# Which engine issues the stores of the squared hidden layer in a hybrid decoder step

## The chip, the cores and the metric

The kernel runs on one core of a Trainium2 chip. The metric is the device time of one execution in microseconds (us), as the median of several runs. The engines are PE (TensorE: matmuls, with PEld for its weight loads), DVE (VectorE), ACT (ScalarE), POOL (GpSimd) and SP (SyncE, which here only waits and issues DMAs). Each engine works off its own list of instructions in order, and an instruction that waits holds back all behind it on that engine. Waits are on semaphores.

## The reference, cut to what matters

One inference step of a one-layer decoder, for 512 prompt tokens and 8 sample tokens, 520 columns in all, with a model width D of 2048: sparse attention and retention side by side, an output projection, then a squared-ReLU MLP and a last RMSNorm. The change lies in the MLP:

```
u = rmsnorm(x, norm2_g) @ w_up            # w_up 2048 x 8192
x = x + jnp.square(jax.nn.relu(u)) @ w_down   # w_down 8192 x 2048
return rmsnorm(x, final_norm_g)
```

All data are float32. Precision is kept by splitting each operand of a product in a high part (a rounded copy, `_hi`, fp32r) and a low part (the rest, `_lo`); a product is three matmuls: hi by hi, hi by lo, lo by hi.

## The kernel before, in words

**The up-projection** goes in 32 groups (g = 0 to 31, `UPG` = 32) of 256 hidden units. The 2 x 2 block product (two halves of the 2048 inputs by two halves of the units, for two halves of 260 tokens) is done with seven products in place of eight, after Strassen and Winograd: DVE makes sums of weight blocks (`sum_blocks`, in PSUM tiles "banks"), and the results are combined afterwards. So a group (from group 1 on) has seven positions, 0 to 6. Each is 24 matmuls of 128 x 260 on PE (`product`, line 907). For each position ACT casts the weights to `w_hi` (`high_unit`, line 1206), and POOL (positions 0, 1, 5, line 578) or DVE (2, 3, 4, 6: `low_sum`, line 1795) subtracts to get `w_lo`.

**PSUM banks** of a group: position 0 writes bank 2 or 0 (by the parity of g), and position 2 adds to the same bank once ACT has copied what position 0 left there (`taken(g, 0, ...)`, line 1251, into `c_b`). PE waits for that copy ahead of position 2 (`s_ra`). The last product of a group is read by ACT's Relu into `r21` at the start of the next group.

**The squares.** After group g - 1, and so during group g, ACT makes the Relus and squares (`relu_rest`, `squared`), DVE combines them to seven block combinations `h_f` (`combine_hidden`, lines 1815 to 1818), ACT makes `h_hi` (`hidden_high`, line 1278) and DVE, last in its list of the group, `h_lo` (`hidden_low`, line 1825). Each of these is 128 x 1820 numbers. Both are then stored to DRAM (`hidden_combinations`, two DMAs of 910 KB) by `store_hidden`. `s_hl` counts the `h_lo` that are done, `s_store` the stores that have landed (32 a group). ACT's `hidden_high(g)` waits for the stores of group g - 1 to have landed, since `h_hi` is a single buffer.

**SP's list** in the up-projection, for each g from 1: wait that a raw buffer is free and load the first half of the weights of group g + 1 (`half_free`, `load_half`, line 430; 1 MB), the same for the second half, then `store_hidden(g - 1)`: wait for `s_hl` and issue the two stores (lines 478 and 479). After group 31's round come seven pairs of loads of stored squares for the first chunk of the down-projection (`load_hidden(0, pos)`, line 490, into `s_dn`, which lies where the normed x, `s_up`, was, so that each waits for PE's use of positions in group 31), a load of weights, `store_hidden(31)`, another load of weights, seven pairs for the second chunk, and, once all stores have landed, the reload of x (line 516) into the space that also held `h_f`, `h_hi` and `h_lo`.

**The down-projection** has 32 groups (g = 32 to 63): 8 chunks of 1024 hidden units by 4 groups of 512 output columns, with seven positions each, of two times 12 matmuls. DVE adds every result to x (`add_down`, line 1865); from the second group on these adds need the x reloaded last.

**ACT's list** in group g: the cast for position 2, Relu of `r21`, Relu of `c_b`, the cast for position 3, the three squares, the copy of `c_b` from position 0, the casts for 4 and 5, a copy, the cast for 6, a copy, the cast for position 0 of group g + 1, `hidden_high(g - 1)`, the cast for position 1 of group g + 1. The functions at the heart of it, as the kernel before has them:

Of the kernel before, what the change touches and what calls it, by code (L numbers as in the profile page):

```python
# [45 lines left out]
UPG, DNG = DFF // HB, NCHUNK * (D // 512)  # L46
# [9 lines left out]
F32, F32R, BF16, I32 = mybir.dt.float32, mybir.dt.float32r, mybir.dt.bfloat16, mybir.dt.int32  # L56
# [10 lines left out]
def base_unit(g):  # L67

    return TAKEN0_UNITS + (4 + 7 * (g - 1) if g else 0)


def ring_slot(n):

    down = base_unit(UPG)
    if n >= down:
        order = (1, 2, 0, 3)
        k = n - down
        return order[k % 4], n - 4 if k >= 4 else (n - 3 if k < 3 else None)
    k = n - TAKEN0_UNITS
    return (k + 2) % 3, n - 3 if k >= 3 else (130, 132, 133)[k]  # L80


def raw_slot(j):

    return (j + 1) % RAWS, 16 * (j // RAWS + 1)
# [38 lines left out]
def build(nc, x_prompt, x_sample, cache_k, cache_v, cache_idx_k, state_ret, page_table, norm1_g, w_in,  # L124
# [3 lines left out]
    with ctx:  # L128
        BASE = 16512

        def at(name, offset, shape, dt=F32):
            return nc.alloc_sbuf_tensor_at(name, shape, dt, offset=BASE + offset)
# [29 lines left out]
        h_hi = at("h_hi", R0 + 11392 + 7296, [P, 7, HALF_COLS], F32R)  # L162
        h_lo = at("h_lo", R0 + 11392 + 14592, [P, 7, HALF_COLS], F32R)
# [108 lines left out]
        h_dram = nc.dram_tensor("hidden_combinations", (P, UPG, 2, 7, HALF_COLS), F32).ap()  # L272
# [4 lines left out]
        def block_of(g, i, j):  # L277

            slot, _ = raw_slot(2 * g + i)
            if g < UPG:  # L280
                return raw[:, slot, :].rearrange("p (k c) -> p k c", c=2 * P)[:, :, j * P:(j + 1) * P]
            return raw[:, slot, :].rearrange("p (k c) -> p k c", c=4 * P)[:, :, 2 * j * P:2 * (j + 1) * P]

        def sums_in(g, n):

            if g < UPG:
                return (T0, T1)[n]
            if g >= LAST_CHUNK and n == 0:
                return t_s[:, :, :]
            return (T0W, T1W)[n]  # L290

        def ring(w, g, n):
            slot, _ = ring_slot(n)
            x = w[:, slot, :, :]
            return x if g < UPG else x.rearrange("p k c -> p (k c)").rearrange("p (k c) -> p k c", c=2 * P)
# [4 lines left out]
        def last_x(g):  # L300

            return 2 if g % 2 else 0
# [54 lines left out]
        def _(sp):  # L357
# [61 lines left out]
            def load_half(g, i):  # L419

                slot, _ = raw_slot(2 * g + i)
                if g < UPG:
                    dst = raw[:, slot, :].rearrange("p (k c) -> p k c", c=2 * P)
                    src = w_up[1024 * i:1024 * i + 1024, HB * g:HB * g + HB].rearrange("(k p) c -> p k c", p=P)
                else:
                    c, w = divmod(g - UPG, D // 512)
                    dst = raw[:, slot, :].rearrange("p (k c) -> p k c", c=4 * P)
                    src = w_down[1024 * c:1024 * c + 1024, 512 * w:512 * w + 512].rearrange(
                        "(k two p) c -> two p k c", two=2, p=P)[i]
                sp.dma_start(dst, src).then_inc(s_h[slot], 16)  # L430

            def half_free(g, i):

                if 2 * g + i < 2:
                    return
                if 2 * g + i == 2:
                    sp.wait_ge(s_lo, TAKEN0_UNITS)
                    return
                before, which = divmod(2 * g + i - RAWS, 2)
                if before == 0:  # L440
                    sp.wait_ge(s_lo, pool_lows(0, 2 + 2 * which))
                elif which == 0:
                    sp.wait_ge(s_lo, pool_lows(before, 1))
                    sp.wait_ge(s_t, 4 * (before - 1) + 3)
                else:
                    sp.wait_ge(s_lo, pool_lows(before, 3))
                    sp.wait_ge(s_t, 4 * (before - 1) + 4)
# [24 lines left out]
            half_free(1, 1)  # L472
            load_half(1, 1)

            def store_hidden(g):

                sp.wait_ge(s_hl, g + 1)
                sp.dma_start(h_dram[:, g, 0, :, :], h_hi[:, :, :].bitcast(F32)).then_inc(s_store, 16)
                sp.dma_start(h_dram[:, g, 1, :, :], h_lo[:, :, :].bitcast(F32)).then_inc(s_store, 16)

            def load_hidden(c, pos):

                if c >= 2:
                    sp.wait_ge(s_used, base_unit(UPG + 4 * (c - 2) + 3) + pos + 1)
                else:
                    sp.wait_ge(s_used, base_unit(UPG - 1) + (pos // 2, (7 + pos) // 2)[c] + 1)
                if c >= 1:
                    sp.wait_ge(s_sd[pos], 32 * c)
                for n in range(2):
                    sp.dma_start(s_dn[:, c % 2, pos, n, :, :].bitcast(F32),  # L490
                                 h_dram[:, 4 * c:4 * c + 4, n, POS_STORE[pos], :]).then_inc(s_sd[pos], 16)

            for g in range(1, UPG):
                half_free(g + 1, 0)
                load_half(g + 1, 0)
                half_free(g + 1, 1)
                load_half(g + 1, 1)
                store_hidden(g - 1)
                if g == UPG - 4:
                    for n in range(2):  # L500
                        sp.wait_ge(s_xs[n], 16 * (5 - n))
                    sp.wait_ge(s_slp, 2)
                    sp.wait_ge(s_sl, 7)
                    sp.dma_start(xr[:, 0:5, :], x2_dram[:, 0:5, :]).then_inc(s_xl[0], 16)
# [2 lines left out]
                load_hidden(0, pos)  # L507
            half_free(UPG + 1, 0)
            load_half(UPG + 1, 0)
            store_hidden(UPG - 1)  # L510
            half_free(UPG + 1, 1)
            load_half(UPG + 1, 1)
            for pos in range(7):
# [519 lines left out]
        def _(act):  # L1033
# [154 lines left out]
            def high_unit(g, pos):  # L1188

                n = base_unit(g) + pos  # L1190
                _, before = ring_slot(n)
                if before is None:
                    act.wait_ge(s_sqh, UPG)
                else:
                    act.wait_ge(s_used, before + 1)
                raw_of = {0: (0, 0), 1: (0, 1), 2: (1, 0), 3: (1, 1)} if g == 0 else {0: (0, 0), 1: (1, 0), 5: (1, 1)}
                if pos in raw_of:
                    i, j = raw_of[pos]
                    slot, loaded = raw_slot(2 * g + i)
                    act.wait_ge(s_h[slot], loaded)  # L1200
                    x = block_of(g, i, j)
                else:
                    which, summed = {2: (1, 2), 3: (0, 1), 4: (0, 3), 6: (1, 4)}[pos]
                    act.wait_ge(s_t, 4 * (g - 1) + summed)
                    x = sums_in(g, which)
                nc.scalar.copy(ring(w_hi, g, n), x).then_inc(s_hi, 1)  # L1206
# [39 lines left out]
            def taken(g, pos, dst, b, fn=None):  # L1246

                act.wait_ge(s_used, base_unit(g) + pos + 1)
                act.wait_ge(s_sqh, g)
                src = G[:, b, 0:HALF_COLS]  # L1250
                (act_fn(dst, src, fn) if fn else nc.scalar.copy(dst, src)).then_inc(s_ra, 1)

            def relu_rest(g):

                act.wait_ge(s_rv, 3 * g)
                act_fn(c_b[:, :, :], c_b[:, :, :], ACT.Relu).then_inc(s_r0, 1)
# [16 lines left out]
            def hidden_high(g):  # L1273

                act.wait_ge(s_comb, g + 1)
                if g:
                    act.wait_ge(s_store, 32 * g)
                nc.scalar.copy(h_hi[:, :, :], h_f[:, :, :]).then_inc(s_hh, 1)

            for g in range(1, UPG):  # L1280
                x_bank = last_x(g)
                high_unit(g, 2)
                if g > 1:
                    taken(g - 1, 6, r21[:, :], last_x(g - 1), ACT.Relu)
                    relu_rest(g - 1)
                high_unit(g, 3)
                squared(g - 1)
                taken(g, 0, c_b[:, 0, :], x_bank)
                high_unit(g, 4)
                high_unit(g, 5)  # L1290
                taken(g, 2, c_b[:, 1, :], x_bank)
                high_unit(g, 6)
                taken(g, 3, c_b[:, 2, :], 3)
                high_unit(g + 1, 0)
                hidden_high(g - 1)
                high_unit(g + 1, 1)
            g = UPG
            taken(g - 1, 6, r21[:, :], last_x(g - 1), ACT.Relu)
            high_unit(g, 2)
# [1 line left out]
            squared(g - 1)  # L1301
            high_unit(g, 3)
            hidden_high(g - 1)

            def squares_of(i):

# [684 lines left out]
```

## Time and profile before

| | us |
|---|---|
| median of 3 runs (2442.13 to 2445.2) | 2444.73 |
| the profiled execution, its own time | 2438.56 |
| its span in the profile | 2436.8 |
| PE busy with matmuls (share of the span) | 2330.6 (96%) |
| DVE / ACT / POOL busy | 1595.0 / 937.6 / 869.7 |
| mean granted clock of PE | 0.975 |

All numbers of the profile belong to the one profiled execution; times are counted from its span's start. A line number names a line of the kernel. "SPq" and "ACTq" are the lists of SP and ACT as far as they issue DMAs, which isn't counted as busy time. A granted clock of 1.00 is PE's upper level of 2.4 GHz, 0.50 its lower one of 1.2 GHz. In the chain of waits "issue" is time in which the engine waited for nothing that the profile shows.

### The profile page before, as it was taken

The numbers are of one execution on the slowest core, as the hardware profiler recorded it, in microseconds if no ns is written. First come the engines' busy times: TensorE is split into PE (matmuls) and PEld (weight loads), VectorE is DVE, ScalarE is ACT, GpSimd is POOL, SyncE is SP. The second block draws the span as 40 slices with busy tenths as digits, with TensorE's granted clock in tenths as the row PEclk, the third lists the DMA queues.
The fourth block names the chain that finished last, engine by engine and source line by source line (L and its number), as shares of the span: only waits on it lengthen the run. The fifth ranks groups of instructions, "written<-read, shape, count | busy, mean of one in ns | idle before, by whom it ended". The sixth has DMA issues, their size and how long they took to land.

```text
span 2436.8 us, 46019 instructions
## 1 busy us (share of the span) xinstructions
PE 2330.6 (96%) x18396; PEld 2257.3 (93%) x18396; DVE 1595.0 (65%) x2316; ACT 937.6 (38%) x1213; POOL 869.7 (36%) x357
## 2 busy tenths in 40 slices
PE   8999999999999999889999999998599999999996
PEld 8969899999999899889999999998599999999996
DVE  5368625555555643488888888888377777777764
ACT  5241222222222322245555555555133333333343
POOL 3413323332333444243333333333133333333353
PEclk9999989999999999899999999999799999999998
DMA  6523223333333443325555555565935556555621
GB/s 217 141 65 102 80 73 89 91 91 91 87 87 86 147 121 113 112 66 197 197 197 197 197 197 197 197 210 201 372 106 192 192 175 227 192 192 175 227 87 71
DMA packets 347063, 368.77 MB, mean 151 GB/s; under 512 B 16594, under 2 KB 301458, under 8 KB 345746
## 3 DMA queue, kind: packets, MB, share of 16 engines
q1 hardware_dynamic: 334850, 352.16, 45.3%
q10 hardware_dynamic: 12064, 14.53, 1.6%
q8 instruction: 105, 1.72, 0.3%
q14 instruction: 44, 0.36, 0.0%
HBM read 288.85 MB, written 77.80 MB: 150 GB/s over the span
## 4 chain that ended last, share of the span: by engine, by line
PE 90%; DVE 4%; DMA 2%; issue 2%; ACT 1%; SPq 1%; POOL 0%; ACTq 0%; DVEq 0%
PE product L907 51%; PE product L618 31%; PE banks L649 6%; PE banks L646 1%; DVE s_up L1738 1%; DMA raw<-in_w_down_dram 1%; DMA x_in<-in_x_prompt_dram 1%; DMA raw<-in_w_up_dram 0%; PE product L649 0%; DVE xr L1732 0%; DMA s_dn<-hidden_combinations 0%; DVE a_lo L1687 0%; SPq L490 0%; DVE xr L1756 0%; DVE score L1504 0%
## 5 line engine op out<-in xcount | busy, mean ns | idle before, releaser
L578 POOL TENSOR_TENSOR w_lo<-raw,w_hi 128x1024 fp32r<-128x1024 f32 x193 | 499.7, 2595 | 852.7 <-ACT w_hi L1206 852.0
L907 PE MATMUL product<-s_dn,w_hi 128*128 128x260 f32 x3584 | 662.8, 287 | 38.0 <-DVE xr L1865 25.1
L907 PE MATMUL product<-s_up,w_hi 128*128 128x260 f32 x3600 | 653.9, 284 | 17.1 <-ACT c_b L1042 8.0
L907 PEld LDWEIGHTS product<-s_dn,w_hi 128*128 128x128 f32 x3584 | 561.8, 191 | 41.7 <-issue 33.7
L907 PEld LDWEIGHTS product<-s_up,w_hi 128*128 128x128 f32 x3600 | 556.8, 189 | 21.5 <-issue 14.2
L545 POOL TENSOR_TENSOR w_lo<-w_raw,w_hi 128x1024 fp32r<-128x1024 f32 (+1 forms) x134 | 323.6, 2417 | 659.0 <-ACT w_hi L1039 658.9
L907 PE MATMUL product<-s_dn,w_lo 128*128 128x260 f32 x1792 | 511.4, 285 | 0.0
L907 PE MATMUL product<-s_up,w_lo 128*128 128x260 f32 x1800 | 508.5, 282 | 0.0
L618 PE MATMUL product<-a_hi,w_hi 128*128 128x260 f32 (+1 forms) x2144 | 440.1, 286 | 7.8 <-DVE a_lo L1396 3.9
L618 PE MATMUL product<-a_hi,w_lo 128*128 128x260 f32 (+1 forms) x2144 | 433.7, 284 | 0.0
L618 PE MATMUL product<-a_lo,w_hi 128*128 128x260 f32 (+1 forms) x2144 | 432.8, 284 | 0.0
L1206 ACT CAST w_hi<-banks 128x1024 fp32r<-128x1024 f32 x244 | 247.6, 1015 | 468.6 <-PE product L907 242.9
L1039 ACT CAST w_hi<-w_raw 128x1024 fp32r<-128x1024 f32 (+1 forms) x134 | 139.6, 1043 | 576.5 <-PE product L618 427.6
L1795 DVE TENSOR_TENSOR w_lo<-banks,w_hi 128x1024 fp32r<-128x1024 f32 x244 | 298.0, 1221 | 74.9 <-ACT w_hi L1206 74.0
L618 PEld LDWEIGHTS product<-a_hi,w_hi 128*128 128x128 f32 (+1 forms) x2144 | 331.8, 189 | 15.2 <-issue 8.1
L907 PEld LDWEIGHTS product<-s_dn,w_lo 128*128 128x128 f32 x1792 | 342.2, 191 | 0.0
L907 PEld LDWEIGHTS product<-s_up,w_lo 128*128 128x128 f32 x1800 | 340.4, 189 | 0.0
L618 PEld LDWEIGHTS product<-a_hi,w_lo 128*128 128x128 f32 (+1 forms) x2144 | 331.5, 189 | 0.0
L618 PEld LDWEIGHTS product<-a_lo,w_hi 128*128 128x128 f32 (+1 forms) x2144 | 330.6, 188 | 0.0
L1865 DVE TENSOR_TENSOR xr<-xr,product 128x260 f32<-128x260 f32 x448 | 188.0, 421 | 181.4 <-PE product L907 157.6
L1206 ACT CAST w_hi<-raw 128x1024 fp32r<-128x1024 f32 x193 | 202.8, 1051 | 233.7 <-PE product L907 200.5
L1789 DVE TENSOR_TENSOR banks<-banks,raw 128x1024 f32<-128x1024 f32 x122 | 149.4, 1224 | 6.0 <-DMA raw<-in_w_down_dram 5.3
(270 smaller groups left out, 1905.9 us busy)
## 6 DMA issues: line engine op xcount, KB each, us to landing
raw<-in_w_up_dram SPq DMA_DIRECT2D x64, 1024.0 KB, 9.6
raw<-in_w_down_dram SPq DMA_DIRECT2D x64, 1024.0 KB, 5.3
s_dn<-hidden_combinations SPq DMA_DIRECT2D x112, 520.0 KB, 8.7
w_raw<-in_w_in_dram SPq DMA_DIRECT2D x100, 512.0 KB, 3.8
hidden_combinations<-h_hi SPq DMA_DIRECT2D x32, 910.0 KB, 3.8
hidden_combinations<-h_lo SPq DMA_DIRECT2D x32, 910.0 KB, 6.8
w_raw<-in_w_out_dram SPq DMA_DIRECT2D x32, 512.0 KB, 4.0
x_transposed<-xr ACTq DMA_DIRECT2D x2, 2080.0 KB, 7.6
```

Of the source, the lines that this page charges most:

```text
L545: nc.gpsimd.tensor_tensor(w_lo[:, slot, :, 0:cols], w_raw[:, raw, :, 0:cols], w_hi[:, slot, :, 0:cols].bitcast(F32), ALU.subtract).then_in ...
L578: nc.gpsimd.tensor_tensor(ring(w_lo, g, n), block_of(g, i, j), ring(w_hi, g, n).bitcast(F32), ALU.subtract).then_inc(s_lo, 1)
L618: last_mm = nc.tensor.matmul(out[:, half, :], w[:, slot, k, 0:cols], a[:, k0 + k, half * HT:(half + 1) * HT], start=(first and k == 0 and ...
L646: return nc.tensor.transpose(out, x, ident[0:n, 0:n])
L649: return nc.tensor.matmul(out, lhsT, rhs, start=start, stop=stop, skip_group_check=True)
L907: mm_last = nc.tensor.matmul(out, w[:, k, col:col + P], s[:, h, k, :], start=(first and k == 0 and part == 0), stop=(last and k == kn - 1 ...
L1039: nc.scalar.copy(w_hi[:, n % RING, :, 0:cols], w_raw[:, n % 2, :, 0:cols]).then_inc(s_hi, 1)
L1206: nc.scalar.copy(ring(w_hi, g, n), x).then_inc(s_hi, 1)
L1738: v.tensor_tensor(s_up[:, pos, 1, ks, :], x[:, ks, :], s_up[:, pos, 0, ks, :].bitcast(F32), ALU.subtract).then_inc(s_sl, 1)
L1789: v.tensor_tensor(out, x, y, ALU.add).then_inc(s_t, 1)
L1795: v.tensor_tensor(ring(w_lo, g, n), sums_in(g, (k + 1) % 2), ring(w_hi, g, n).bitcast(F32), ALU.subtract).then_inc(s_lt, 1)
L1865: v.tensor_tensor(acc, acc, G[:, 2 * sub + pos % 2, 0:HALF_COLS], op).then_inc(s_rd, 1)
```

## The change

`store_hidden` moves from SP's list to ACT's, with its wait and both DMAs. In group g ACT now ends its list, after the cast for position 1 of group g + 1, with `store_hidden(g - 1)`; the last, `store_hidden(31)`, follows `hidden_high(31)`, ahead of the casts of group 32's position 4 and later. SP's list keeps its order without these entries. Nothing else is changed.

```
@@ SP's list
-            def store_hidden(g):
-
-                sp.wait_ge(s_hl, g + 1)
-                sp.dma_start(h_dram[:, g, 0, :, :], h_hi[:, :, :].bitcast(F32)).then_inc(s_store, 16)
-                sp.dma_start(h_dram[:, g, 1, :, :], h_lo[:, :, :].bitcast(F32)).then_inc(s_store, 16)
-
...
                 half_free(g + 1, 1)
                 load_half(g + 1, 1)
-                store_hidden(g - 1)
                 if g == UPG - 4:
...
             half_free(UPG + 1, 0)
             load_half(UPG + 1, 0)
-            store_hidden(UPG - 1)
             half_free(UPG + 1, 1)
             load_half(UPG + 1, 1)
@@ ACT's list
                 nc.scalar.copy(h_hi[:, :, :], h_f[:, :, :]).then_inc(s_hh, 1)
 
+            def store_hidden(g):
+
+                act.wait_ge(s_hl, g + 1)
+                act.dma_start(h_dram[:, g, 0, :, :], h_hi[:, :, :].bitcast(F32)).then_inc(s_store, 16)
+                act.dma_start(h_dram[:, g, 1, :, :], h_lo[:, :, :].bitcast(F32)).then_inc(s_store, 16)
+
...
                 hidden_high(g - 1)
                 high_unit(g + 1, 1)
+                store_hidden(g - 1)
             g = UPG
...
             high_unit(g, 3)
             hidden_high(g - 1)
+            store_hidden(g - 1)
```

## Rows read from the trace of the kernel before

**Rows 1.** The page's busy table: us (share of the span), instructions of each engine.

```profile
PE 2330.6 (96%) x18396; PEld 2257.3 (93%) x18396; DVE 1595.0 (65%) x2316; ACT 937.6 (38%) x1213; POOL 869.7 (36%) x357
```

**Rows 2.** The chain that ended last: start us, us, what.

```profile
1072.90 546.95 PE product L907 x4536
...
1748.92 16.99 issue
```

**Rows 3.** Stretches: us, busy us (instructions) by engine, granted clock, DMA share, GB/s.

```profile
1087.47:1107.72 20.25, 20.25 (x170) 20.12 (x170) 17.52 (x17) 11.95 (x16) 7.85 (x4) 1.00 0.59 197
...
1699.80:1765.90 66.10, 32.35 (x216) 31.80 (x216) 19.53 (x29) 10.34 (x11) 7.12 (x3) 0.73 1.06 369
```

**Rows 4.** Timeline, SP and ACT at the hand-over: start, us, engine, line, [idle before <-releaser].

```profile
1679.92 3.76 SPq L430 DMA_DIRECT2D raw<-in_w_down_dram  x2
...
1696.17 0.39 ACT L1042 ACTIVATE r<-product 128x260 f32<-128x260 f32 x1 [1.81 <-PE product L907]
...
1699.78 21.16 SPq L490 DMA_DIRECT2D s_dn<-hidden_combinations  x14
...
1724.92 26.76 SPq L490 DMA_DIRECT2D s_dn<-hidden_combinations  x14
...
1751.73 1.41 SPq L516 DMA_DIRECT2D xr<-x_after_attention  x1
```

**Rows 5.** Timeline of the engines at one boundary of groups, 1103 to 1114 us.

```profile
1103.15 5.46 POOL L578 TENSOR_TENSOR w_lo<-raw,w_hi 128x1024 fp32r<-128x1024 f32 x2 [3.33 <-ACT w_hi L1206]
...
1106.37 4.15 DVE L1825 TENSOR_TENSOR h_lo<-h_f,h_hi 128x1820 fp32r<-128x1820 f32 x1
...
1107.76 1.01 ACT L1206 CAST w_hi<-banks 128x1024 fp32r<-128x1024 f32 x1 [1.81 <-PE product L907]
1108.67 0.39 ACT L1042 ACTIVATE r<-product 128x260 f32<-128x260 f32 x1
...
1110.62 1.02 ACT L1206 CAST w_hi<-banks 128x1024 fp32r<-128x1024 f32 x1 [0.82 <-PE product L907]
...
1111.46 4.06 SPq L430 DMA_DIRECT2D raw<-in_w_up_dram  x2
...
1112.88 0.38 ACT L1251 COPY c_b<-product 128x260 f32<-128x260 f32 x1
...
1113.17 0.28 PE L907 MATMUL product<-s_up,w_lo 128*128 128x260 f32 x1
1113.40 0.48 PE L907 MATMUL product<-s_up,w_hi 128*128 128x260 f32 x2
```

**Rows 6.** Line 1825, h_lo: count, duration in ns min/median/max, first and last start.

```profile
L1825 DVE TENSOR_TENSOR h_lo<-h_f,h_hi x32: 2044/4142/4149, 1086.1 to 1707.7; 128x1820 fp32r<-128x1820 f32 x32
```

**Rows 7.** Waits from 1072.9 to 1696.1, SP and PE: us, times, longest.

```profile
SPq L478 <- DVE h_lo L1825: 456.3, 30, 15.4
...
PE product L907 <- ACT c_b L1251: 2.3, 1, 2.3
```

**Rows 8.** Timeline of ACT about its own output stores in the attention stage.

```profile
388.51 0.37 ACTq L1162 DMA_DIRECT2D out_dram<-rst  x1
...
389.46 1.28 ACT L1042 ACT_TABLE_LOAD   x1 [0.88 <-issue]
```

**Rows 9.** Stretches at gaps of PE, columns as in group 3.

```profile
1072.90:1076.31 3.41, 3.41 (x28) 3.41 (x29) 2.28 (x3) 1.29 (x2) 0.00 (x0) 1.00 0.19 50
...
2365.69:2368.30 2.61, 0.00 (x0) 0.03 (x1) 1.11 (x3) 1.40 (x4) 0.00 (x0) 1.00 0.75 290
2368.30:2371.71 3.41, 3.41 (x16) 3.33 (x17) 0.00 (x0) 1.54 (x3) 1.98 (x2) 0.51 0.00 0
```

**Rows 10.** The chain again: 24 products after gaps of PE, and undisturbed.

```profile
2369.56 3.92 PE product L907 x24
...
2374.03 2.89 PE product L907 x24
...
2396.09 4.30 PE product L907 x24
```

More of the change, by code:

```diff
@@ L473, in _ @@
             load_half(1, 1)
[L475 to L479, printed above, removed]
             def load_hidden(c, pos):
@@ L497, in _ @@
                 load_half(g + 1, 1)
-                store_hidden(g - 1)
                 if g == UPG - 4:
@@ L509, in _ @@
             load_half(UPG + 1, 0)
-            store_hidden(UPG - 1)
             half_free(UPG + 1, 1)
@@ L1278, in hidden_high, with store_hidden @@
                 nc.scalar.copy(h_hi[:, :, :], h_f[:, :, :]).then_inc(s_hh, 1)
+            def store_hidden(g):
+                act.wait_ge(s_hl, g + 1)
+                act.dma_start(h_dram[:, g, 0, :, :], h_hi[:, :, :].bitcast(F32)).then_inc(s_store, 16)
+                act.dma_start(h_dram[:, g, 1, :, :], h_lo[:, :, :].bitcast(F32)).then_inc(s_store, 16)
             for g in range(1, UPG):
@@ L1296, in _ @@
                 high_unit(g + 1, 1)
+                store_hidden(g - 1)
             g = UPG
@@ L1303, in _ @@
             hidden_high(g - 1)
+            store_hidden(g - 1)
             def squares_of(i):
```

## The prediction

> **What bounds the kernel now.** I read the page's busy table first. The matmuls of TensorE (PE) are busy for 96% of the span, and no other engine above 65% [rows 1]. The chain of waits then says where PE is left alone. One piece of it is 546.95 us of products from 1072.90 on, without a gap: nearly the whole up-projection, the stage in which the squares are stored. In the hand-over to the down-projection the same chain is broken, longest by "issue 16.99" from 1748.92 to 1765.91, a stretch in which the view names nobody [rows 2].
>
> The change touches both places, so I asked of each what ends last there. In the hand-over it is the memory: from 1699.80 to 1765.90 the DMA engines have a share of 1.06 at 369 GB/s [rows 3], and PE stands again when x comes back, whose reload was issued last, at 1751.73, behind 28 loads of stored squares [rows 4]. In the steady groups I laid the engines' own rows beside each other at one boundary: ACT's first cast of the new group follows PE's last unit of the old one at 1107.76 [rows 5]. A group takes 20.25 us, with PE busy for 20.25 [rows 3].
>
> **What SP is relieved of.** In the up-projection SP stood 30 times and 456.3 us in all for DVE's h_lo, ahead of the store of h_hi [rows 7]: 15.2 us in each group. The loads queued behind it were not late for PE, since nothing in that piece of the chain waits for them [rows 2]. In the steady groups this removes idle time of an engine with slack, and I cost it at nothing.
>
> **What ACT takes on.** The wait moves with its two issues. ACT now stands, at the end of each group's list, for the h_lo of the group before. Behind it is queued the next group's list: the cast for position 2, Relu of r, Relu of c_b, the cast for position 3, three squares, and the copy of c_b that frees the PSUM bank which PE writes again at position 2.
>
> When is h_lo ready? DVE starts it at 1106.37 and it takes 4.15 us, so it ends at 1110.52 [rows 5], 2.76 us after ACT began the new group. That is every group's case: of 32 such instructions the median takes 4142 ns, and the shortest 2044 [rows 6]. It is long because POOL's two subtractions run until 1108.61 [rows 5]; from there to 1110.52 it is 1.91 us, close to the short form. Both POOL pieces follow casts that ACT does ahead of the new wait, so I leave the end at 1110.52.
> The Trainium skill, "SBUF — State Buffer" (section "SBUF: two separate sides"), says that a VectorE instruction with two SBUF inputs waits wholly while a GpSimd instruction reads SBUF: a lock, not a shared bandwidth. The trace agrees: with half the rate during the 2.24 us of overlap h_lo would have taken 3.2 us, not 4.15. By shared bandwidth the stall below would be 0.95 us smaller.
>
> What do the issues cost? From h_lo's end at 1110.52 SP needs until 1111.46 to come to its next load, signal and both stores included: 0.94 us [rows 5]. ACT's own pair of output stores, at 388.51, lets its next instruction begin at 389.46: 0.95 us [rows 8]. I take 0.94.
>
> So ACT begins the group at 1111.46 and not at 1107.76: 3.70 us late. What covers it? ACT idled 0.82 us ahead of the cast for position 3, and an instruction with nothing to wait for starts 0.1 us before the last one ends (1108.67 against 1107.76 + 1.01) [rows 5]: 0.9 us together. There is no second reserve. The copy of c_b runs from 1112.88 to 1113.26, and PE's position 2 began at 1113.40, 0.23 us after the matmul before it, where 0.12 is the usual distance [rows 5]: PE already waits 0.11 us for this copy. What is beyond the 0.9 us is PE's idle time: 3.70 - 0.90 = 2.8 us. DVE's w_lo for position 2 would be ready at 1111.46 + 1.01 + 1.2 = 1113.7 and is not the later one. After position 2 the group moves as one: h_lo hangs on PE's position 5, through DVE's work on c_b, so the next boundary finds the same distances and nothing is made up.
>
> The stores of groups 0 to 29 delay groups 2 to 31: 30 x 2.8 = 84 us. The bounds for one group are 0, if ACT finds a cover that I don't see, and 3.70, if none of the 0.9 us can be used; I take 2.8, since each piece has its row, with 2.5 to 3.0 about it.
>
> **The clock.** PE's gap becomes 2.8 + 0.11 = 2.9 us in each group of about 23. The trace has gaps near that. After one of 2.61 us at 2365.69 the granted clock was 0.51 over the next 3.41 us (and the same came after its twin at 2392.60), but in the up-projection it was 1.00 after a gap of 2.3 us [rows 9], which is the very wait in question: PE for the copy of c_b, in the first group [rows 7]. After the two falls 24 products took 3.92 and 4.30 us instead of 2.89 [rows 10], dearer by 1.03 and 1.41, on average 1.2. With two of three gaps followed by the lower level, 1.2 GHz, that is 0.8 us a group and 24 us in all. Bounds: 0, and half of 3.41 us, 1.7, in every group, 51 us.
>
> **The hand-over.** SP passes straight from the loads of group 32's weights to the loads of the squares. The last of the former was issued by 1679.92 + 3.76 = 1683.68, the first of the latter at 1699.78, after SP's wait for h_lo [rows 4], 16.1 us apart. Their own condition, that PE has used positions of group 31, is met by then or a few us on, and they read groups 0 to 3, stored long before. The stretch is one of bandwidth and 66.1 us long. It begins 16.1 us earlier against PE's end of group 31 and has one load of 1 MB more inside, 2.8 us at 369 GB/s: a gain of 13.3, say 13. What is late next? ACT comes into the stretch 3.7 us late, and its last h_hi waits until the store of group 30 has landed, which now runs beside loads. By the durations above, position 2 of group 32 starts 15 to 20 us after PE's end of group 31 (that was about 1696.1, when `r<-product` starts on ACT [rows 4]), with some 20 us of products to go before x is needed. x comes at 56 us (1765.9 - 1696.1 - 13), so this is covered. Bounds for the gain: 0 and 20.
> The Trainium skill, "DMA: Bandwidth & Descriptors" ("Issuing engines are not separate DMA queues"), says that DMAs of different engines interleave on the same 16 engines, so that a second issuer only saves time on the first one's sequencer. By that rule the second queue adds no bandwidth and the gain is that of the order alone. No row before the change has stores of ACT beside saturated loads of SP. Its section on the anatomy of a DMA adds that a semaphore wait is made on the issuing sequencer: SP's 456.3 us are such waits, and they are what speaks against ACT as the issuer.
>
> **The sum**, against the profiled execution (2438.56 us, span 2436.8): 84 + 24 - 13 = +95, that is 2533.6. The median of the three timed runs lies 6.2 us higher, at 2444.73. With that difference: 2540 us.
>
> **Rivals.**
> (a) The stall comes, and the clock stays high, as after the 2.3 us gap: +84 - 13 = +71, 2516. For it speaks that one case; against it, that the new gap is longer than all three.
> (b) The clock falls in every group: +84 + 51 - 13 = +122, 2567. Against it: both prices read are under 1.7.
> (c) The other side: the wait on ACT is covered and only the hand-over changes, 2444.7 - 13 = 2432. Its one mechanism is that h_lo is done before ACT comes to the store. To cost nothing it must end by 1107.76 + 0.9 - 0.94 = 1107.7, 2.8 us sooner than now. Against it: even the short form, from 1106.37, ends at 1108.4, and would leave 0.7 us a group (+21 - 13 = +8).
> (d) The change does nothing: the loads of squares stay where they are, and the wait on ACT is short. 2445; the rows name no cause for either.
>
> **Chances.** The forecast 0.62 (its own range 2525 to 2560), (a) 0.20, (b) 0.12, (c) 0.04, (d) 0.02. The range that should hold 8 in 10 reaches from (a) with 2.5 us a group to a little beyond (b): 2505 to 2572. About 0.2% (5 us) is what a measurement of this kernel can tell: slower 0.94, within it 0.02, faster 0.04.
>
> **What would show it.** Right: PE idle about 2.9 us at position 2 in each of 30 groups, on ACT's copy of c_b or what stands behind it; ACT waiting some 2.8 us a group for DVE's h_lo, or for its queue of two stores; groups of 23 to 24 us; a granted clock under 1.00 in the up-projection; SP's wait for h_lo gone and its first load of squares ahead of PE's end of group 31; the hand-over 13 us shorter. Wrong: groups of 20.25 us again; a stall of PE on w_lo or on a weights' load; a hand-over as long as before, because the last stores wait beside the loads.

## The result, and the profile after

The changed kernel takes 2537.75 us (median of 4 runs, 2534.43 to 2539.63) against 2443.43 us before: ratio 1.0391, 95% interval 1.0378 to 1.0404. It is slower by 94 us. The forecast was 2540, 95 us more than before.

The page after has PE at 93% of a longer span (96% in [rows 1]); no other engine has a larger share than before. PE's own busy time grew by 31.5 us, with the same number of products, because some of them ran at the lower clock.

```profile
span 2534.9 us, 46019 instructions
...
PE 2362.1 (93%) x18396; PEld 2287.1 (90%) x18396; DVE 1610.6 (64%) x2316; ACT 934.4 (37%) x1213; POOL 863.2 (34%) x357
```

To find where the 98.1 us between the two spans lie, I cut both executions at the same events: PE's resumption after its wait of some 8 us in group 0, PE's start of position 2 of group 2 and of group 31, and PE's resumption when x is back. These are the stretches of the kernel before (columns as in [rows 3]).

```profile
0.00:1061.99 1061.99, 1021.26 (x7712) 957.40 (x7713) 565.03 (x1084) 309.65 (x436) 353.68 (x153) 0.98 0.36 104
1061.99:1093.15 31.16, 28.89 (x217) 28.58 (x217) 26.10 (x19) 16.18 (x25) 14.60 (x5) 0.91 0.19 62
1093.15:1681.57 588.42, 587.53 (x4874) 583.63 (x4873) 505.87 (x464) 346.44 (x464) 228.53 (x87) 1.00 0.60 199
1681.57:1766.48 84.91, 46.92 (x337) 46.18 (x337) 36.13 (x45) 20.46 (x23) 14.93 (x6) 0.79 0.94 327
1766.48:2436.80 670.32, 645.99 (x5260) 641.54 (x5260) 461.81 (x705) 244.84 (x266) 257.94 (x107) 0.97 0.50 167
```

And these of the changed one:

```profile
0.00:1064.83 1064.83, 1023.67 (x7712) 959.22 (x7713) 563.47 (x1084) 310.09 (x436) 353.29 (x153) 0.98 0.36 104
1064.83:1101.29 36.46, 30.27 (x216) 29.91 (x217) 24.66 (x20) 16.07 (x25) 14.28 (x5) 0.86 0.33 110
1101.29:1795.56 694.27, 620.14 (x4872) 614.88 (x4873) 523.68 (x465) 342.96 (x464) 222.27 (x87) 0.95 0.50 168
1795.56:1867.11 71.55, 44.56 (x337) 43.91 (x337) 36.21 (x45) 20.48 (x23) 15.32 (x6) 0.83 1.02 359
1867.11:2534.90 667.79, 643.50 (x5260) 639.18 (x5260) 462.59 (x705) 244.76 (x266) 258.06 (x107) 0.98 0.50 167
```

The differences are +2.84, +5.30, +105.85, -13.36 and -2.53 us, which add up to +98.1. The 29 groups in the third stretch lose 105.85 us, and the hand-over gives back 13.36, with the same number of products on PE. The first and the last stretch hold nothing that the change touches, and vary by 3 us either way. Of the second's 5.30 us, 1.3 belong to group 1, which the change doesn't touch either (PE from product to product 3.88 us there, 2.55 before).

What PE waits for in the up-projection was one wait before [rows 7]. Now (the view of waits from 1075.7 to 1795.6):

```profile
PE product L899 <- ACT c_b L1243: 80.3, 31, 3.6
```

That is once in each group, and always on the copy of c_b. The timeline of one boundary, the one to set against [rows 5], shows why. Lines: DVE's h_lo, ACT's list, then PE.

```profile
1236.22 3.96 DVE L1825 TENSOR_TENSOR h_lo<-h_f,h_hi 128x1820 fp32r<-128x1820 f32 x1
...
1240.22 0.33 ACTq L1275 DMA_DIRECT2D hidden_combinations<-h_hi  x1
1240.58 0.45 ACTq L1276 DMA_DIRECT2D hidden_combinations<-h_lo  x1
1241.12 1.02 ACT L1198 CAST w_hi<-banks 128x1024 fp32r<-128x1024 f32 x1 [5.32 <-PE product L899]
...
1243.06 1.01 ACT L1198 CAST w_hi<-banks 128x1024 fp32r<-128x1024 f32 x1
...
1245.31 0.38 ACT L1243 COPY c_b<-product 128x260 f32<-128x260 f32 x1
...
1243.05 0.28 PE L899 MATMUL product<-s_up,w_lo 128*128 128x260 f32 x1
1245.83 0.77 PE L899 MATMUL product<-s_up,w_hi 128*128 128x260 f32 x2 [2.50 <-ACT c_b L1243]
```

h_lo ends at 1240.18, the two stores go out behind it, ACT's first cast starts 0.94 us after h_lo's end, the next cast has no idle time before it any more, and PE starts position 2 at 1245.83, 2.78 us after its last product and not 0.23. (Where the clock hadn't fallen since the gap before, it is 2.94 to 2.99.) A lesson on reading: the view puts ACT's 5.32 us of idle time down to PE, the condition of the cast itself. What held ACT is the wait of the store in front of it, and the order of the rows shows that: the DMA issues come first.

After these gaps the clock falls, but not after all. Two stretches, each from one start of position 2 to the next:

```profile
1198.42:1221.45 23.03, 20.35 (x168) 20.17 (x169) 17.74 (x17) 11.83 (x16) 7.84 (x3) 1.00 0.51 173
1221.45:1245.83 24.38, 21.88 (x169) 21.70 (x169) 18.14 (x17) 11.82 (x16) 7.71 (x3) 0.92 0.48 164
```

Of the 29 such groups 8 take 23.02 us on average at a clock of 1.00, and 21 take 24.29 with a fall to the lower level in them. In the hand-over SP's first load of squares now goes out at 1797.58, ahead of PE's end of group 31 at about 1810; in [rows 4] it came 3.6 us behind that end. The timeline of SP there:

```profile
1797.16 0.37 SPq L430 DMA_DIRECT2D raw<-in_w_down_dram  x1
1797.58 23.41 SPq L484 DMA_DIRECT2D s_dn<-hidden_combinations  x14
1821.10 8.70 SPq L430 DMA_DIRECT2D raw<-in_w_down_dram  x2
1829.89 22.43 SPq L484 DMA_DIRECT2D s_dn<-hidden_combinations  x14
1852.38 1.41 SPq L508 DMA_DIRECT2D xr<-x_after_attention  x1
```

### The profile page after: what moved, and what is told of

Read it like the earlier page. It is cut to its first block and busy times, and to the rows that moved or that the text cites. A ratio compares the mean times of both kernels' runs of the same rounds, so it can differ in the third digit from the quotient of the medians.

```text
span 2534.9 us, 46019 instructions
## 1 busy us (share of the span) xinstructions
PE 2362.1 (93%) x18396; PEld 2287.1 (90%) x18396; DVE 1610.6 (64%) x2316; ACT 934.4 (37%) x1213; POOL 863.2 (34%) x357
## 5 line engine op out<-in xcount | busy, mean ns | idle before, releaser
L570 POOL TENSOR_TENSOR w_lo<-raw,w_hi 128x1024 fp32r<-128x1024 f32 x193 | 493.6, 2560 | 955.4 <-ACT w_hi L1198 954.3
L899 PE MATMUL product<-s_up,w_hi 128*128 128x260 f32 x3600 | 685.3, 292 | 94.0 <-ACT c_b L1243 80.3
L899 PEld LDWEIGHTS product<-s_up,w_hi 128*128 128x128 f32 x3600 | 583.8, 198 | 99.8 <-DVE w_lo L1795 85.9
L899 PEld LDWEIGHTS product<-s_dn,w_hi 128*128 128x128 f32 x3584 | 559.0, 190 | 30.5 <-issue 16.5
L899 PE MATMUL product<-s_up,w_lo 128*128 128x260 f32 x1800 | 523.2, 291 | 0.0
L899 PEld LDWEIGHTS product<-s_up,w_lo 128*128 128x128 f32 x1800 | 355.2, 197 | 0.0
```

Source lines behind the costliest of these rows:

```text
L570: nc.gpsimd.tensor_tensor(ring(w_lo, g, n), block_of(g, i, j), ring(w_hi, g, n).bitcast(F32), ALU.subtract).then_inc(s_lo, 1)
L899: mm_last = nc.tensor.matmul(out, w[:, k, col:col + P], s[:, h, k, :], start=(first and k == 0 and part == 0), stop=(last and k == kn - 1 ...
```

## The experiments

**1. The stores on ACT, at another place.** (`e1_later_place` in the expectations.) All stores stay ACT's, but each stands in the next group, behind the copy of c_b. The edit is to the changed kernel.

```
                 high_unit(g + 1, 1)
-                store_hidden(g - 1)
...
                 taken(g, 0, c_b[:, 0, :], x_bank)
+                if g > 1:
+                    store_hidden(g - 2)
...
             relu_rest(g - 1)
+            store_hidden(g - 2)
             squared(g - 1)
```

> ACT issues all stores, on its own queue, but the store of group g-2 stands in group g right behind the copy of c_b from position 0 (h_lo has long been done there, and ACT idles 1.9 us before its next cast); the store of group 30 stands ahead of the squares of group 31, which wait for the same h_lo. Theory (the loss is ACT standing in front of the store while h_lo isn't ready, plus the two issues ahead of the copy): groups of 20.25 us again, PE's wait for the copy gone, granted clock 1.00, and the hand-over about 13 us shorter than before, so 2430 us. Rival 1 (a second queue beside the loads, or stores issued by ACT, is dear in itself): the loss stays in good part, over 2480. Rival 2 (the two issues, not the wait, are what costs): some 0.9 us a group stay, +28, so about 2458.

Measured: 2429.07 us, ratio to before 0.9946 (0.9933 to 0.9960). The issues fall in ACT's idle time ahead of the cast for position 4:

```profile
1235.48 0.38 ACT L1243 COPY c_b<-product 128x260 f32<-128x260 f32 x1
1235.51 0.33 ACTq L1275 DMA_DIRECT2D hidden_combinations<-h_hi  x1
1235.86 0.46 ACTq L1276 DMA_DIRECT2D hidden_combinations<-h_lo  x1
1237.76 1.01 ACT L1198 CAST w_hi<-banks 128x1024 fp32r<-128x1024 f32 x1 [1.90 <-DVE banks L1791]
```

The groups take 20.25 to 20.31 us, as they do in experiment 2, where SP issues these stores. A second queue and ACT as the issuer cost nothing measurable at this place; both rivals fall. The loss comes from where in its list ACT waits and issues.

**2. Only the last two stores on ACT.** (`e2_last_two`.) The edit is shown against the kernel before.

```
                 load_half(g + 1, 1)
-                store_hidden(g - 1)
+                if g < UPG - 1:
+                    store_hidden(g - 1)
...
-            store_hidden(UPG - 1)
... ACT's list, for the last two alone
+                if g == UPG - 1:
+                    store_last(g - 1)
...
             hidden_high(g - 1)
+            store_last(g - 1)
```

> Only the last two stores (groups 30 and 31) are issued by ACT as in the change; the thirty before stay with SP. Theory (steady groups lose by ACT's wait, the hand-over gains by SP passing on to the loads of squares): no stall in groups 2 to 31, the gain of the hand-over of 13 us alone, so 2430. Rival (the hand-over gained nothing by itself, the 13 us of difference are the phase of the clock or another accident): 2443, as before.

Measured: 2430.36 us, 0.9951 (0.9937 to 0.9965). The gain of the hand-over stands alone. In the trace, from PE's last product of group 31 to its resumption with x, it is 60.1 us here, 70.6 before and 57.3 in the changed kernel.

**3. Only the wait on ACT.** SP keeps all stores.

```
                 high_unit(g + 1, 1)
+                act.wait_ge(s_hl, g)
```

> The kernel before, in which SP issues all stores, and ACT only waits for the h_lo of group g-1 at the end of group g, where the change has the store. Theory: of the 2.6 us that the stall adds in a group of the changed kernel, 0.9 are the two issues, so the wait alone adds 1.7 us in each of 30 groups, 51 us, and no gain in the hand-over; with the clock as high as before 2494, with it falling as often as in the change 2525. I take 2494 to 2525. Rival (the queue or the issues are what costs, the wait is covered): 2443 to 2450.

Measured: 2498.43 us, 1.0236 (1.0218 to 1.0253), in the interval given and near its lower end. The groups take 22.10 us each, so the wait alone adds 1.85 us of the 2.77 of the changed kernel (23.02 - 20.25), and the two issues the other 0.92. By [rows 5] they were 1.86 (2.76 - 0.90) and 0.94. The view of waits from 1110 to 1750, PE and ACT, names here what the changed kernel's hid:

```profile
PE product L907 <- ACT c_b L1251: 50.8, 29, 1.8
...
ACT w_hi L1206 <- DVE h_lo L1826: 132.5, 29, 4.6
```

PE stands 2.03 us from product to product, and the clock never fell in the up-projection's groups. One of them:

```profile
1110.93:1133.03 22.10, 20.35 (x171) 20.17 (x170) 17.71 (x17) 11.82 (x16) 7.82 (x4) 1.00 0.53 180
```

**4. The gap filled.** The changed kernel with 18 products more in each of groups 2 to 30, whose result nobody reads, ahead of PE's wait. PE's wait for position 2's weights (`made`) moves behind them, so that they don't wait for `w_lo`.

```
-                    made(g, pos)
+                    if not (pos == 2 and 2 <= g < UPG - 1):
+                        made(g, pos)
...
+                    if pos == 2 and 2 <= g < UPG - 1:
+                        for _ in range(18):
+                            nc.tensor.matmul(bank(1), s_up[:, 0, 0, 0, 0:P], s_up[:, 0, 0, 1, :], start=True,
+                                             stop=True, skip_group_check=True)
+                        made(g, pos)
                     if pos in (2, 4, 5):
                         pe.wait_ge(s_ra, ...)
```

> The changed kernel, with 18 matmuls more on PE (2.2 us, into a PSUM bank that nobody reads) in groups 2 to 30 ahead of PE's wait for the copy of c_b, so that PE's idle time there shrinks to some 0.6 us while the wait ends when it did. Theory (of the 109 us lost in the up-projection 31 are the low clock after the gaps): the stall to the next product stays at 2.8 to 2.9 us, the granted clock is 1.00 through the up-projection, and the time falls by 31 to about 2507. Rival (the products are slower after the gap for another reason, or the low clock costs nothing net): 2537, as the change.

Measured: 2514.06 us (2507.10 to 2516.76), ratio to before 1.0289 (1.0268 to 1.0309), so 24 us less than the change, where 31 were expected. More work on PE made the kernel faster. The row over the up-projection and one group:

```profile
1101.00:1760.00 659.00, 641.42 (x5302) 636.42 (x5301) 506.23 (x459) 336.14 (x453) 226.16 (x87) 1.00 0.51 174
...
1109.51:1132.51 23.00, 22.48 (x189) 22.30 (x188) 17.71 (x18) 11.83 (x16) 7.81 (x4) 1.00 0.50 173
```

The groups take 23.00 us, as the changed kernel's with no fall. The changed kernel's 21 falls at 24.29 - 23.02 = 1.27 us are 27 us, and 24 of them came back; the 31 of my expectation counted the stall too low. Part of the missing 3 us is in this trace: three groups were longer, 23.75, 26.31 and 25.47 us, each behind an issue of ACT's store of h_lo that took longer than its median of 0.45 us (1.20, 2.22 and 1.34):

```profile
L1282 ACTq DMA_DIRECT2D hidden_combinations<-h_lo x32: 450/452/2221, 1090.7 to 1801.2; - x32
```

The longest issue left a gap of 2.57 us in spite of the filling; the last of the three stands ahead of group 31, which has no filling, and left 3.85. After both the clock fell.

**5. The mirror of 2.** ACT has the stores of groups 0 to 29, SP the last two: in the changed kernel's lists the condition `if g < UPG - 1` stands before ACT's store, and SP's two last stores are back.

> The mirror of e2_last_two: the stores of groups 0 to 29 are ACT's as in the change, the last two are SP's as before. Theory (the two effects add): the stalls of 30 groups as in the change less nothing, and no gain in the hand-over, so 13 us more than the change: 2551. Rival (the gain of the hand-over needs nothing of the last two stores, or the effects depend on each other): 2538.

Measured: 2549.47 us, 1.0428 (1.0411 to 1.0446): 11.7 us over the change. Experiments 2 and 5 add up: -12.5 for the last two (2430.36 against 2442.88), +106.4 for the others (2549.47 against 2443.09), together +93.9, and the change has +94.3. In this trace the hand-over takes 70.6 us, as before.

**6. Only h_hi on ACT, without a wait for h_lo.** SP's list loses the store of h_hi and keeps its wait and the store of h_lo; ACT's has, at the place of the change:

```
+            def store_high(g):
+                act.wait_ge(s_hh, g + 1)
+                act.dma_start(h_dram[:, g, 0, :, :], h_hi[:, :, :].bitcast(F32)).then_inc(s_store, 16)
```

> The kernel before, but the store of h_hi alone is ACT's, at the place of the change and without a wait for h_lo (h_hi is ACT's own); the store of h_lo stays with SP behind its wait. Theory (an issue of 0.35 us falls in ACT's idle 1.8 us at the end of the group; a queue of ACT's beside the loads costs nothing): as before, 2443, groups of 20.25 us. Rival (stores on ACT's queue cost by themselves at this place): 0.35 us or more a group, 2453 and up.

Measured: 2437.03 us, 0.9969 (0.9957 to 0.9980). The groups are as before (20.30 us), as the theory has it: one issue at this place, without the wait, costs PE nothing. But it is 6 us faster than before, which I had not expected. 2 us of it are in the hand-over: from PE's last product ahead of it to the resumption it is 1697.38 to 1765.94, 68.6 us, against 1695.86 to 1766.48, 70.6. The two profiled executions differ by 3.1 us only (2433.7 against 2436.8): besides these 2, the part behind the resumption is 2.5 shorter, as it is in the changed kernel, and the part ahead of the up-projection 1.4 longer. Where the rest of the 6 us is from stays open.

**7 and 8. The reload of x ahead of the second chunk's squares.** What still holds PE in the hand-over of experiment 1 is x. The edit, on top of it (7, `e6_x_first`) and on the kernel before (8, `e7_x_first_sp`):

```
+            sp.wait_ge(s_store, 32 * UPG)
+            sp.dma_start(xr[:, 5:KT, :], x2_dram[:, 5:KT, :]).then_inc(s_xl[1], 16)
+            ... both halves of group 34's weights
             for pos in range(7):
                 load_hidden(1, pos)
-            sp.wait_ge(s_store, 32 * UPG)
-            sp.dma_start(xr[:, 5:KT, :], x2_dram[:, 5:KT, :]).then_inc(s_xl[1], 16)
```

> e1_later_place, and in SP's list the reload of x stands ahead of the seven pairs of loads for the second chunk (it needs the last stores landed, some 1722 in e1's time), followed by both loads of group 34's weights and then the pairs. Theory (the last wait of the hand-over, 18.2 us of PE in e1, is for the reload behind 7 MB of loads that nobody needs until group 36): that wait goes and no new one of over 3 us comes, 2411. Rival (the stretch is bound by bandwidth, whatever the order; the wait moves to the weights of group 34 or to the squares of group 36): 2420 to 2429.

> The same order of SP's list in the kernel before, whose stores stay with SP. Theory: the wait for x (16 us of PE) goes, but the waits of the hand-over ahead of it (12.9, 4.1 and 4.9 us) stay, so 2443 - 16 = 2427. Rival as for e6_x_first: 2435 to 2443.

Measured: 2408.66 us on top of experiment 1 (0.9858, 0.9839 to 0.9876) and 2426.58 us on the kernel before (0.9925, 0.9911 to 0.9940). The first is faster than both kernels of the case, by 34 us against before. PE's waits from 1690 to 1770, first in experiment 1:

```profile
PE product L899 <- DVE xr L1867: 30.6, 2, 17.9
```

and then in this one:

```profile
PE product L904 <- DVE xr L1872: 12.3, 1, 12.3
```

The 17.9 us on x are gone, and no new wait took their place. Experiment 7 is 20.4 us faster than experiment 1. The rest fits the clock: in experiment 1 it stayed at the lower level for 5.28 us after x had come back, and in experiment 7 it was at 1.00 all that time. The stretch in experiment 1, columns as in [rows 3]:

```profile
1756.40:1761.68 5.28, 5.28 (x24) 5.28 (x25) 4.69 (x7) 1.96 (x2) 2.16 (x1) 0.50 0.57 203
```

The DMA engines are as full as before (a share of 1.07 from 1738.18 to 1765.00 in experiment 7). PE was bound by bandwidth there only because of what stood ahead of x in the queue. On the kernel before, experiment 8 gains 16.5 us, where 16 were expected.

## Why the prediction was right, point by point

- **What SP is relieved of, at nothing.** Right. SP's wait for h_lo is gone, and the loads are issued sooner without any effect in the groups: experiment 1, which has the same SP list, keeps 20.3 us a group. The one late load of the kernel before had not stood behind h_lo: it was issued at 1621.52, when its buffer was free, and took 11.09 us to land; PE came to its product at 1638.11 1.17 us after the one before.
- **The stall, 2.8 us in each of 30 groups.** Right in place, mechanism and size: groups without a fall take 23.02 us, 2.77 over 20.25. Its parts came out as read: 0.94 us from h_lo's end to the cast; the casts for positions 2 and 3 start 1.94 us apart, where it was 2.86, so that the whole reserve of 0.9 was used; the two prices apart in experiment 3, 1.85 for the wait and 0.92 for the issues. No cover was found that the rows hadn't shown.
- **How long h_lo takes.** It kept its long form, 3.96 us at the median where it was 4.14 [rows 6]: 3.96 in groups with a fall of the clock, 4.12 to 4.15 in the eight without. That agrees with the lock of the Trainium skill ("SBUF — State Buffer", "SBUF: two separate sides"). No run took POOL's instruction away, but in one group of the kernel before h_lo began first, by 0.05 us. Then h_lo took its short time and POOL's subtraction 4.24 us, where 2.40 is the median, 1.84 longer. The two rows of that group:

```profile
1633.77 2.04 DVE L1825 TENSOR_TENSOR h_lo<-h_f,h_hi 128x1820 fp32r<-128x1820 f32 x1
1633.82 4.24 POOL L578 TENSOR_TENSOR w_lo<-raw,w_hi 128x1024 fp32r<-128x1024 f32 x1 [0.36 <-ACT w_hi L1206]
```

And h_lo in the changed kernel:

```profile
L1825 DVE TENSOR_TENSOR h_lo<-h_f,h_hi x32: 2054/3962/4147, 1091.6 to 1824.7; 128x1820 fp32r<-128x1820 f32 x32
```

- **The clock, 24 us.** Right, with some luck: falls in 21 of 29 groups (0.72, forecast two of three), at 1.27 us each (forecast 1.2): 27 us for the 29. A share read from three gaps, of which only two were near the new one in length, could hardly be relied on. Rivals (a) and (b), never and always, are both excluded by the same trace. Experiment 4 shows that the falls, and not the gap alone, cost this: with the gap filled 24 us came back. The kernel before has a fourth gap of that kind, which I didn't count, 2.94 us from product to product ahead of 2341.61. The clock was low after it too:

```profile
2341.61:2345.03 3.42, 3.42 (x18) 3.34 (x19) 0.00 (x0) 1.54 (x3) 1.95 (x2) 0.58 0.00 0
```

- **The hand-over, 13 us.** Right: 13.36 in the trace, 12.5 by experiment 2 (10.5 in its trace) and 11.7 by experiment 5. The DMA engines were as full there as before (1.06 at 380 GB/s from 1811.20 to 1866.50, against 1.06 at 369 [rows 3]), so the second queue added little bandwidth, and the earlier start is the gain. That agrees with the Trainium skill ("DMA: Bandwidth & Descriptors", "Issuing engines are not separate DMA queues"), by which DMAs from all issuers run on the same 16 engines. Position 2 of group 32 began at 1828.35, some 18 us behind the end of group 31, inside the 15 to 20 forecast.
- **The sum, 95 us.** Each term was right to a few us: 84 + 24 = 108 for 30 groups, and the trace has 105.85 for 29. That the sum came within 1 us is luck: the two untouched stretches differ by +2.84 and -2.53 us, which happen to cancel.
- **What I missed.** Not in the change but beside it: I took the stretch for one of bandwidth and left it there, when the order of its queue was worth 16 us in the kernel before and 20 on top of experiment 1.
- **Rival (c)**, the other side, failed at the point named for it: h_lo would have had to end 2.8 us sooner.

## What to carry to other kernels

A store costs its issuer two things, the wait for its data and the issue, and on an engine that computes, each counts from where the list stands, not from how idle the engine is: ACT was 38% busy and the move cost 94 us, and the same stores a few instructions further down its list gained 14. Look for the one instruction behind the wait that another engine's next step needs, and add up its reserve from the rows; here it was 0.9 us against 3.7. In a stretch bound by transfers, ask which of them ends the wait and what stands ahead of it that nobody needs yet.

## What the runs showed of the hardware that I had not expected

Gaps of PE that differ by less than a microsecond have quite different prices. After 29 gaps of 2.03 us from product to product (experiment 3) the clock stayed at its upper level; after gaps of 2.78 to 2.99 us in the same measure it fell 21 times of 29, in runs of two to four with one left out between them. All eight gaps of 2.94 us and more were followed by a fall there, and 13 of the 21 shorter ones; experiment 5 has one of 2.94 us without. So a shorter stall gains more than its length: the 0.92 us less per group in experiment 3 are 27 us less stall in 29 groups and another 27 of clock. With the 13 us that experiment 3 lacks in the hand-over that makes 41 us, and 39.3 were measured (2537.75 - 2498.43).
